# Attention units of the first token tile ahead of the second's in a fused mLSTM and sparse-attention layer

## What is computed

```python
q = q.reshape(b_, t_, G, HPG, DH)                 # G = 4 groups of HPG = 4 heads, DH = 128
p_c = softmax(q . k_cmp * scale + bias_c) * mask_c   # 15 compressed key blocks
o_cmp = p_c . v_cmp
p_s = softmax(q . k_sel * scale + bias_s)            # selected blocks: at 256 tokens, all causal ones
o_s = p_s . v_sel
p_w = softmax(q . k_win * scale + bias_w)            # window of 512: again all causal ones
o_w = p_w . v_win
o = gates[..., 0:1] * o_cmp + gates[..., 1:2] * o_slc + gates[..., 2:3] * o_win
y_a = o * silu(a_z)
```

## Time and profile before

| | |
|---|---|
| time, median of 3 executions | 1813.21 us (1812.64 to 1813.79) |
| profiled execution, its own time | 1812.75 us |
| its span | 1811.0 us |
| granted TensorE clock, mean | 0.998 of full speed |
| TensorE matmul busy | 1788.4 us (99%) |
| vector engine busy | 1132.1 us (63%) |
| ScalarE busy | 846.6 us (47%) |
| GpSimd busy | 74.3 us (4%) |

### The profile page before, as it was taken

One profiled execution on the slowest core, in us unless ns is written; L12 is line 12 of the kernel. 1 busy time (PEld: TensorE's weight loads), 2 busy tenths in 40 slices (PEclk: granted clock), 3 DMA queues, 4 the chain that ended last, 5 costly groups with the idle time before them and its releaser, 6 DMA issues.

```text
span 1811.0 us, 23485 instructions
## 1 busy us (share of the span) xinstructions
PE 1788.4 (99%) x8256; PEld 1483.4 (82%) x8256; DVE 1132.1 (63%) x1388; ACT 846.6 (47%) x1158; POOL 74.3 (4%) x54
## 2 busy tenths in 40 slices
PE   9999999999999999999999999999999999999997
PEld 7888888887878878788888888888888888888886
DVE  6546644577685767775667566856684865555454
ACT  7535444455555545543444344434443544444443
POOL 0000000001000010100000000000000000000000
PEclk9999999999999999999999999999999999999999
DMA  9647555545445454455555555555555566666664
GB/s 386 232 149 233 185 187 196 179 160 175 151 158 179 151 176 161 163 164 182 191 195 186 175 196 191 184 179 190 193 187 175 185 243 219 203 205 206 203 205 175
DMA packets 97159, 346.58 MB, mean 191 GB/s; under 512 B 10560, under 2 KB 11200, under 8 KB 96704
## 3 DMA queue, kind: packets, MB, share of 16 engines
q1 hardware_dynamic: 94192, 337.19, 55.5%
q10 hardware_dynamic: 2896, 8.39, 1.4%
HBM read 341.35 MB, written 4.19 MB: 191 GB/s over the span
## 4 chain that ended last, share of the span: by engine, by line
PE 91%; DVE 5%; issue 1%; ACT 1%; DMA 1%; DVEq 0%; SPq 0%; POOL 0%; ACTq 0%; POOLq 0%
PE acc_b L489 15%; PE acc_b L491 15%; PE acc_b L490 15%; PE acc_a L489 13%; PE acc_a L491 13%; PE acc_a L490 13%; DVE w_split L1280 2%; DVE ebuf L1333 1%; DMA w_raw<-in_w_all 1%; PE bank_z L742 1%; PE bank_x L490 0%; PE bank_x L491 0%; PE bank_x L489 0%; PE bank_v L490 0%; PE bank_v L491 0%
## 5 line engine op out<-in xcount | busy, mean ns | idle before, releaser
L1280 DVE TENSOR_TENSOR w_split<-w_raw,w_split 128x1024 fp32r<-128x1024 f32 x619 | 779.1, 1262 | 590.8 <-ACT w_split L905 588.6
L905 ACT ACTIVATE w_split<-w_raw 128x1024 fp32r<-128x1024 f32 x619 | 653.6, 1059 | 789.0 <-PE acc_a L491 386.3
L489 PE MATMUL acc_b<-w_split,lhs_hi 128*128 128x512 f32 x1216 | 477.1, 392 | 0.0
L489 PE MATMUL acc_a<-w_split,lhs_hi 128*128 128x512 f32 x1204 | 474.6, 394 | 1.3 <-DVE w_split L1280 1.3
L491 PE MATMUL acc_b<-w_split,lhs_lo 128*128 128x512 f32 x1216 | 473.5, 389 | 0.0
L490 PE MATMUL acc_b<-w_split,lhs_hi 128*128 128x512 f32 x1216 | 473.5, 389 | 0.0
L491 PE MATMUL acc_a<-w_split,lhs_lo 128*128 128x512 f32 x1204 | 469.1, 390 | 0.0
L490 PE MATMUL acc_a<-w_split,lhs_hi 128*128 128x512 f32 x1204 | 468.9, 389 | 0.0
L491 PEld LDWEIGHTS acc_b<-w_split,lhs_lo 128*128 128x128 f32 x1216 | 228.3, 188 | 48.0
L489 PEld LDWEIGHTS acc_b<-w_split,lhs_hi 128*128 128x128 f32 x1216 | 228.4, 188 | 46.1 <-DVE w_split L1280 0.3
L490 PEld LDWEIGHTS acc_b<-w_split,lhs_hi 128*128 128x128 f32 x1216 | 228.5, 188 | 46.0
(11 more groups left out here) (267 smaller groups left out, 878.6 us busy)
## 6 DMA issues: line engine op xcount, KB each, us to landing
w_raw<-in_w_all SPq DMA_DIRECT2D x615, 512.0 KB
wide<-in_x SPq DMA_DIRECT2D x8, 512.0 KB, 8.9
xres<-in_x ACTq DMA_DIRECT2D x8, 512.0 KB, 4.2
out_y<-wide SPq DMA_DIRECT2D x8, 512.0 KB, 3.2
gained_x<-in_x_cols_first SPq DMA_DIRECT2D x2, 1024.0 KB, 10.7
toe<-in_toe_bias ACTq DMA_DIRECT2D x4, 512.0 KB, 5.2
gain_f<-in_final_norm_gain ACTq DMA_DIRECT2D x1, 2048.0 KB, 14.6
gained_x<-in_x_cols_first SPq DMA_DIRECT2D x2, 512.0 KB, 8.6
```

The lines of the kernel that those rows point to most:

```text
L489: pe.matmul(dst, a[0], b[0], start=start, stop=False)
L905: act.activation(w_hi[:, cols], w_raw[:, cols], ACT.Copy).then_inc(hi_done, 1)
L1280: dve.tensor_tensor(w_lo[:, cols], w_raw[:, cols], w_hi[:, cols].bitcast(F32), ALU.subtract).then_inc(lo_done, 1)
```

## The change

The order of a group's units and the batches. Before, the four units of tile 1 come first, in two batches of two heads, and the four of tile 0 behind them in one batch. After, the four units of tile 0 come first, in one batch of four heads, and the four of tile 1 behind them, in two batches of two. With that `values` stands at slots 16 (tile 0), 22 and 28 (tile 1), where it stood at slots 10 and 16 (tile 1) and 28 (tile 0). Nothing else is changed.

```diff
-UNIT_ORDER = [(hh, 1) for hh in range(HPG)] + [(hh, 0) for hh in range(HPG)]
-BATCHES = ((1, (0, 1), 1), (1, (2, 3), 3), (0, (0, 1, 2, 3), 7))
+UNIT_ORDER = [(hh, 0) for hh in range(HPG)] + [(hh, 1) for hh in range(HPG)]
+BATCHES = ((0, (0, 1, 2, 3), 3), (1, (0, 1), 5), (1, (2, 3), 7))
```

## The result

The changed kernel takes 1821.18 us (median of 5 executions, 1820.26 to 1822.7) against 1813.14 us (5, 1812.58 to 1813.79): ratio 1.0047, 95% interval 1.0032 to 1.0061, so slower by 8.0 us. The forecast was 1817.5 us, slower, with a range up to 1820.8.

The account below looks back on a forecast made before the run. TensorE was taken as full, losing time only where attention-weight transposes wait for the vector engine. Stalls growing about 1.2 us a group, +4.8 over four groups, on 1812.75 gave 1817.5 us, range 1814.2 to 1820.8.

Parts of the forecast that it names:

- Step 2: Unit 4 to 5 in each group: chain 10.59 us against 9.64 TensorE needs; lost 0.95, before 0.07.
- step 3: Unit 5 to 6: vector chain 10.52 us, TensorE 11.19 with the moved values batch; nothing lost, before 0.44.
- step 4: Unit 6 to 7: chain 12.06 us against 9.64, GpSimd's product delaying the second split; lost 2.42, before 1.60.
- step 5: First half of each group, now tile 0: chain at most 8.24 us against 9.12 needed; nothing lost.
- the two splits at 4.41: Vector splits beside GpSimd's gate product, unit 6 to 7: still 4.41 us in place of 2.21.
- The sum of the stalls: Per group: 3.37 us lost after, 2.11 before, about +1.2; four groups +4.8 us.
- The upper bound: Moved values batch covers nothing at unit 5 to 6: 0.88 us more lost, +2.1 a group, 1821.2 us.
- The lower bound: Longer transposes and copy (+0.44 us) hidden at units 4 to 5 and 6 to 7: +0.35 a group, 1814.2 us.
- The rival "no change": Whole kernel: TensorE's work is the same, so no measurable difference, 1813 to 1816.8 us; chance 0.27.
- The delay that runs on: Vector engine falls back until pairs wait for their own split: 1 to 2 us more a group, 1822 to 1826; chance 0.03.
- the order in which both splits go ahead of GpSimd's product: Splits at slots 24 and 25: 2.2 us vanish per group, kernel faster at 1808.7 us; chance 0.06.

Follow-up runs that it names:

- e2: Changed kernel with GpSimd's gate product started only after the last unit's weights are done: 1808.63 us, ratio 0.9976.
- e3: Kernel before the change, with GpSimd's gate product started only after the last unit's weights are done: 1806.33 us, ratio 0.9965.
- e7: The third order with GpSimd's gate product started only after the last unit's weights are done: 1805.95 us, ratio 0.996.
- e8: The third order with the gate's last reciprocal, and so GpSimd's product, at slot 27 in place of 24: 1804.85 us, ratio 0.9952.
- e1: Changed kernel with eight spare matmuls per group ahead of the wait for the last unit's attention weights: 1818.35 us, ratio 1.003.
- the third order: Changed kernel reordered: two heads of tile 1, four of tile 0, two of tile 1; values at slots 10, 22, 28: 1815.37 us.
- e9: Changed kernel with four spare matmuls in the stall ahead of unit 5's transposes, the longer stall left: 1822.86 us, ratio 1.0051.
- e4: The run of the third order without further edits, timed beside the kernel before: 1815.37 us, ratio 1.0014.

## Why the prediction was right and wrong

Right: the direction, and each chain. Step 2 (10.59 worked out, 10.55 in the trace), step 3 (no stall at unit 6, the batch of slot 22 covers it; the vector engine's chain 10.49 against 10.52; TensorE's 11.31 against 11.19, of which 0.06 is the slower run of the transposes behind the stall at unit 5, 0.66 against 0.60 us), step 4 (12.06 and 12.04), step 5 (nothing lost in the first half: 9.11, 9.15 and 9.11 us between units 0 to 3 in group 1), the two splits at 4.41. The sum of the stalls, +1.2 a group, is the +1.18 of the group without a fall. e2, e3, e7 and e8 bear the terms out: 1808.63, 1806.33, 1805.95 and 1804.85 measured, 1809.2, 1806.7, 1805.5 and 1804.7 worked out.

Wrong: the size, and with it the range. The step that failed is step 4, "Lost 2.42, before 1.60": it priced the longer stall by its length alone. TensorE's idle time there grew to 2.7 us, and behind it the clock fell in two groups of the profiled execution, 1.59 us each, which no term, bound or rival had. e1 showed it: the same chain with the idle time filled has no fall and gains 3.0 us within the groups. The kernel before, with idle times of up to 1.9 us at the same place, had no fall in its trace, so no row of it priced one; but its full clock was a premise of the sum that the prediction did not state, and with a stall half as long again it should have been a bound: 1 to 4 falls at the price of a few matmuls at half clock.

The upper bound, 1821.2, from which the range took 1820.8, held a case (the moved batch covers nothing) that did not come, and not the one that did. That 1821.2 is the measured time is luck: four times 0.88 us for a batch without use happens to be near twice 1.59 us for the clock. The lower bound (the +0.44 hidden) fell as well. The rival "no change" is out: TensorE is the fullest engine at 98%, and shifting vector work still cost 8 us. The delay that runs on, and the order in which both splits go ahead of GpSimd's product, did not occur; when the product was put elsewhere by hand (e2), the 2.2 us came back in each group; that rival's 1808.7 and e2's 1808.63 rest on the same term.

Open: how many falls an execution has and why the third order has fewer (0 to 2 or so by the clock) than the changed kernel with the same last stall; and why eight spare matmuls a group cost 0.7 us at other units of the kernel before and 0.9 us behind its groups.

## What to carry to other kernels

Where one engine is full and others wait their turn beside it, look at which units stand beside the other engines' side work, and read the chain from one release to the next, row by row: each came out within 0.05 us. But price a growing stall of TensorE twice, by its length and by what the clock does behind it. And before changing the order, look at what lies over the chain: moving one GpSimd product by about two slots, or the reciprocal that releases it by three, was worth 6 to 7 us on the kernel before; with the product out of the way, the three orders of the units that were tried lie within 3 us of each other, and the quickest of them has two of the heavy units at the end, since the `values` batch at slot 22 covers a stall.

## What the hardware showed unexpectedly

An idle time of 2.7 us was followed by half clock in some groups and not in others with the same rows ahead of it (groups 0 and 2 in one kernel, 2 and 3 in e9, one of four in e4), at a price of 1.59 us where it was read. The half clock did not begin with the first matmul behind the stall but 1.1 to 1.7 us later. Behind the stalls of up to 1.9 us in the groups of the kernel before it never came in the trace. Spare matmuls with results thrown away kept the clock up, at a price of their own of 2.2 us on the kernel before.
